# A fused transformer block on one core: cross attention written out head by head, x's tiles turned tile by tile at the layer borders, and the memory and bias transfers cut into pieces

## The reference, cut to what matters

```python
x = x + rms_norm(mixed, mix_post_g[l])
h = rms_norm(x, cross_pre_g[l])
m = rms_norm(mem, mem_norm_g[l])
qx = (h @ w_cq[l]).reshape(B, S, CX_HEADS, CX_HEAD_DIM)        # 4 heads of 128
kv = (m @ w_ckv[l]).reshape(B, M, 2, CX_HEADS, CX_HEAD_DIM)    # keys, values
s = jnp.einsum('bqhd,bkhd->bhqk', qx, kv[:, :, 0]).astype(jnp.float32) * CX_HEAD_DIM ** -0.5
p = jax.nn.softmax(s, axis=-1)
o = jnp.einsum('bhqk,bkhd->bqhd', p.astype(x.dtype), kv[:, :, 1]).reshape(B, S, CX_WIDTH)
x = x + rms_norm(o @ w_co[l], cross_post_g[l])
h = rms_norm(x, ffn_pre_g[l])
```

## Time and profile before

| what | us |
|---|---|
| median of 3 runs (2542.57 to 2543.47) | 2543.34 |
| the profiled execution | 2544.24 |
| its span, first to last instruction | 2542.4 |
| PE busy | 2493.5 (98%) |
| DVE busy | 1422.9 |
| ACT busy | 1222.6 |
| POOL busy | 23.3 |

### The profile page before, as it was taken

The page is one execution under the profiler, slowest core; times in us unless marked ns, Lnnn a source line. Parts: engine busy times, 40 slices in busy tenths (PEclk is TensorE's granted clock), DMA queues, the critical chain, the costliest instruction groups (busy, mean ns, idle before and its releaser), DMA issues.

```text
span 2542.4 us, 32059 instructions
## 1 busy us (share of the span) xinstructions
PE 2493.5 (98%) x11995; PEld 2080.1 (82%) x11995; DVE 1422.9 (56%) x1921; ACT 1222.6 (48%) x1699; POOL 23.3 (1%) x43
## 2 busy tenths in 40 slices
PE   8999999998999999999999999999999999999998
PEld 6788887877888888888888898887888888888887
DVE  4468887664645455454445655676654544544444
ACT  5645457654544444444445555554544444443443
POOL 1000000000000000000000000000000000000000
PEclk9999999997999999999999999999999999999999
DMA  7855444552556556655564775333565555556664
GB/s 239 244 178 159 151 145 158 165 190 85 187 186 190 188 190 190 190 186 194 191 196 150 229 222 177 105 123 127 161 196 189 190 190 190 190 186 207 195 191 157
DMA packets 238580, 456.07 MB, mean 179 GB/s; under 512 B 16468, under 2 KB 24916, under 8 KB 237712
## 3 DMA queue, kind: packets, MB, share of 16 engines
q1 hardware_dynamic: 234896, 440.92, 54.3%
q0 software_dynamic: 3584, 13.79, 1.8%
HBM read 449.40 MB, written 5.24 MB: 179 GB/s over the span
## 4 chain that ended last, share of the span: by engine, by line
PE 93%; DVE 3%; DMA 1%; ACT 1%; issue 1%; POOL 0%; DVEq 0%; ACTq 0%; POOLq 0%
PE g L310 23%; PE g L312 23%; PE g L311 23%; PE g L953 4%; PE g L955 4%; PE g L954 4%; PE g L1864 1%; DMA raw<-in_w_in 1%; PE g L1866 1%; PE g L1868 1%; PE m L983 1%; DVE wl L298 1%; PE m L706 1%; PE m L616 1%; ACT wh L294 0%
## 5 line engine op out<-in xcount | busy, mean ns | idle before, releaser
L298 DVE TENSOR_TENSOR wl<-raw,wh 128x1024 fp32r<-128x1024 f32 (+1 forms) x836 | 1015.1, 1220 | 939.4 <-ACT wh L294 936.5
L294 ACT ACTIVATE wh<-raw 128x1024 fp32r<-128x1024 f32 (+1 forms) x836 | 879.0, 1056 | 1114.6 <-PE g L312 919.8
L310 PE MATMUL g<-wh,act_hi 128*128 128x512 f32 x1824 | 720.0, 395 | 9.6 <-DVE wl L298 4.6
L311 PE MATMUL g<-wl,act_hi 128*128 128x512 f32 x1824 | 713.6, 391 | 0.0
L312 PE MATMUL g<-wh,act_lo 128*128 128x512 f32 x1824 | 713.5, 391 | 0.0
L310 PEld LDWEIGHTS g<-wh,act_hi 128*128 128x128 f32 x1824 | 344.6, 189 | 83.3 <-DVE act_lo L643 5.5
L312 PEld LDWEIGHTS g<-wh,act_lo 128*128 128x128 f32 x1824 | 344.7, 189 | 73.0
L311 PEld LDWEIGHTS g<-wl,act_hi 128*128 128x128 f32 x1824 | 345.1, 189 | 69.9
L310 PE MATMUL g<-wh,ht_hi 128*128 128x512 f32 x688 | 267.8, 389 | 0.0
L312 PE MATMUL g<-wh,ht_lo 128*128 128x512 f32 x688 | 267.7, 389 | 0.0
L311 PE MATMUL g<-wl,ht_hi 128*128 128x512 f32 x688 | 267.6, 389 | 0.0
(11 more groups left out here) (363 smaller groups left out, 2188.6 us busy)
## 6 DMA issues: line engine op xcount, KB each, us to landing
raw<-in_w_ffn_in SPq DMA_DIRECT2D x176, 512.0 KB, 3.4
raw<-in_ffn_w_in SPq DMA_DIRECT2D x176, 512.0 KB, 3.5
raw<-in_w_in SPq DMA_DIRECT2D x112, 512.0 KB, 4.3
raw<-in_w_ffn_out SPq DMA_DIRECT2D x88, 512.0 KB, 3.7
raw<-in_ffn_w_out SPq DMA_DIRECT2D x88, 512.0 KB, 3.6
raw<-in_nsa_w_in SPq DMA_DIRECT2D x80, 512.0 KB, 4.4
raw<-in_w_out SPq DMA_DIRECT2D x32, 512.0 KB, 4.6
raw<-in_nsa_w_out SPq DMA_DIRECT2D x32, 512.0 KB, 4.6
```

Of the source, the lines that this page charges most:

```text
L294: nc.scalar.activation(wh[:, j % SLOTS, 0:n], raw[:, j % SLOTS, 0:n], ACT.Copy).then_inc(hi_done, 1)
L298: nc.vector.tensor_tensor(wl[:, j % SLOTS, 0:n], raw[:, j % SLOTS, 0:n], wh[:, j % SLOTS, 0:n].bitcast(F32), ALU.subtract).then_inc(lo_don ...
L310: nc.tensor.matmul(dst, h, whk, start=(first and k == 0), stop=False)
L311: nc.tensor.matmul(dst, h, wlk, start=False, stop=False)
```

## The change

1. **Order of mx.** The query units are now 108 to 115, between the values' 104 to 107 and 116 to 119 (`CW_0`). x's first bank is transposed after unit 106 and not after 107; ACT's squares of x come after its conversion of unit 116.
2. **Queries** are multiplied with the weights stationary (24 matmuls of 256 columns a unit), so that they come out transposed; x's norm goes into the scale of the exponential. x's second half has its own tiles `xt_hi`, `xt_lo`.
3. **Cross attention** is written out for four heads without a loop and without POOL. Keys are transposed after unit 92, scores come behind unit 116, the softmax runs beside units 117 to 119, the values are multiplied so that co's operand comes out directly, and DVE writes the value rows of p1 ahead of its conversions of co's units.
4. **Borders.** Turned tiles of x go on one by one: PE waits for the first tile's high part and then for its low part (`pe_first_unit`, at in1f, ff1, in2c, ff2); the two tiles stand in different PSUM banks (`turn_rows`). co and fo1 are skewed as well; ACT squares tile 0 while tile 1 is multiplied, and loads the table of the square root ahead.
5. **Transfers.** `mem` comes in 4 pieces of 512 KB, the masks behind them, the bias rows are written in 12 pieces of 256 KB; each piece waits for a unit of in1q or mx. ACT's squares of `mem` move to units 26 and 27 of in1q.

```diff
+        def act_last_squares(act, name, junk, then, early):
+
+            s = gemms[name]
+            c = s["chunks"] - 1
+            for j in range(early):
+                act_unit(act, gemms[then]["u0"] // SLOTS, j)
+            for t in range(T):
+                act.wait_ge(*((tile_used, SKEWED[name]) if t == 0 else (unit_used, used(s, c))))
+                nc.scalar.activation(junk[:, c % 2, t, :], g[:, 2 * (c % 2) + t, :], ACT.Square, accum_out=ss8[:, t, c:c + 1])\
+                  .then_inc(ss_done, 1)
+                if t == 0:
+                    for j in range(early, AHEAD):
+                        act_unit(act, gemms[then]["u0"] // SLOTS, j)
...
-            u0 = s["units"] - SLOTS
+            n = min(SLOTS, s["units"])
+            u0, end = s["units"] - n, s["u0"] + s["units"] * s["chunks"]
             for t in range(T):
-                for j in range(SLOTS):
-                    slot = (s["u0"] + s["units"] * s["chunks"] - SLOTS + j) % SLOTS
-                    pe.wait_ge(lo_done, SLOTS + s["u0"] + s["units"] * s["chunks"] - SLOTS + j + 1)
...
+        def pe_first_unit(pe, name, cyc, hi, lo):
+
+            pe.wait_ge(lo_done, SLOTS + cyc * SLOTS + 1)
+            for k in range(2):
+                whk, wlk = wh[:, 0, k * NB:(k + 1) * NB], wl[:, 0, k * NB:(k + 1) * NB]
+                pe.wait_ge(*((first_hi, FIRST[name] + 1) if k == 0 else (hi_evac, BANKS[name] + 1)))
+                for t in range(T):
+                    h = hi[:, k, t * P:(t + 1) * P]
+                    nc.tensor.matmul(g[:, t, :], h, whk, start=(k == 0), stop=False)
+                    nc.tensor.matmul(g[:, t, :], h, wlk, start=False, stop=False)
+                pe.wait_ge(*((first_lo, FIRST[name] + 1) if k == 0 else (lo_evac, BANKS[name] + 1)))
+                for t in range(T):
+                    ins = nc.tensor.matmul(g[:, t, :], lo[:, k, t * P:(t + 1) * P], whk, start=False, stop=False)
+            ins.then_inc(unit_used, 1)
+
...
 
+        def turn_rows(name, b, k):
+
+            bank = BANKS[name] + b + (2 if k and b == 0 and name in FIRST else 0)
...
+                    26: mem_squares_first, 27: mem_squares(1, junk_m1), 29: lambda: act_sqrt(act, "nmem")}
...
+            if c == CQ:
+                for k in range(2):
+                    x_hi, x_lo = (tile_of("ncx", b, 2 * u + k) for b in (act_hi, act_lo))
+                    for h in range(CX_H):
+                        w0 = k * NB + h * P
+                        dst = g[:, 2 * (c % 2) + h // 2, h % 2 * S:(h % 2 + 1) * S]
+                        nc.tensor.matmul(dst, wh[:, n % SLOTS, w0:w0 + P], x_hi, start=(2 * u + k == 0 and h % 2 == 0), stop=False,
+                                         skip_group_check=True)
+                        nc.tensor.matmul(dst, wl[:, n % SLOTS, w0:w0 + P], x_hi, start=False, stop=False, skip_group_check=True)
+                        ins = nc.tensor.matmul(dst, wh[:, n % SLOTS, w0:w0 + P], x_lo, start=False, stop=(2 * u + k == 15),
+                                               skip_group_check=True)
...
+            pe_cx_keys(pe)
+            for n in range(O1_0 + 5, CV_0 + 3):
+                pe_mx_unit(pe, n)
+            pe.wait_ge(cx_keyed, 2)
+            pe_turn_bank(pe, "ncx", 0)
+            pe_mx_unit(pe, CV_0 + 3)
+            pe_turn_bank(pe, "ncx", 1)
             for j in range(8):
-                if j + 5 < 8:
-                    pe_turn_bank(pe, "ncx", j + 5)
                 pe.wait_ge(lo_evac, BANKS["ncx"] + j + 1)
                 pe_mx_unit(pe, CQ_0 + j)
+                if j + 2 < 8:
+                    pe_turn_bank(pe, "ncx", j + 2)
+            pe_mx_unit(pe, CW_0)
+            for h in range(CX_H):
+                pe_cx_scores(pe, h)
+            for n in range(CW_0 + 1, MX_UNITS):
+                pe_mx_unit(pe, n)
+            for h in range(CX_H):
+                pe_cx_back(pe, h)
+            for h in range(CX_H):
+                pe_cx_values(pe, h)
...
+            act_mx_unit(act, CW_0)
             act.wait_ge(x_done, ADDED["ncx"][1] + 16)
-            act_squares(act, "ncx", x, [junk_x[:, 0, :], junk_x[:, 1, :]])
-            act_mx_unit(act, CQ_0 + 4)
...
+            act_mx_unit(act, CW_0 + 2)
             act_sqrt(act, "ncx")
-            act_mx_unit(act, CQ_0 + 6)
-            act_mx_unit(act, CQ_0 + 7)
-            ahead(act_unit, act, "co")
-            act_mx_evict(act, CQ, MX_UNITS - 1)
-            act_unit(act, gemms["co"]["u0"] // SLOTS, AHEAD)
+            act_cx_queries(act)
+            act_mx_unit(act, CW_0 + 3)
+            act_unit(act, gemms["co"]["u0"] // SLOTS, 0)
+            for h in range(CX_H):
+                act_cx_exp(act, h)
+            for j in (1, 2):
+                act_unit(act, gemms["co"]["u0"] // SLOTS, j)
+            for h in range(CX_H):
+                act_cx_weights(act, h)
...
-        cx_banks, cx_q, cx_k, cx_qk, cx_p, cx_w = [m, g], [xq_s, xq_s1], [xk_s, xk_s1], [xqk, xqk1], [xp, xp1], [xpt, xpt1]
+            dve_cx_scale(dve)
+            dve_mx_unit(dve, CW_0 + 3)
+            dve_cx_top(dve, 0)
+            dve_cx_top(dve, 1)
+            dve_cx_soft(dve, 0)
+            dve_cx_top(dve, 2)
+            dve_cx_soft(dve, 1)
+            dve_cx_top(dve, 3)
+            dve_cx_soft(dve, 2)
+            dve_cx_soft(dve, 3)
+            dve_cx_rows(dve)
+            ahead(dve_unit, dve, "co")
+            for h in range(CX_H):
+                dve_cx_lo(dve, h)
+            dve_unit(dve, gemms["co"]["u0"] // SLOTS, AHEAD)
...
-        def pool_cx(pool):
-            pool.wait_ge(pair_free[CQ % 2], mx_pair[CQ % 2] + CQ // 2 + 2)
-            pool.wait_ge(pair_free[CKV_V % 2], mx_pair[CKV_V % 2] + CKV_V // 2 + 2)
-            with pool.Fori(0, CX_H // 2) as i:
...
-            for l in LANES:
-                pe.sem_inc(cx_turned[l], 1)
-            with pe.Fori(0, CX_H // 2) as i:
...
+            pe.wait_ge(pair_free[0], mx_freed(8))
+            pe.wait_ge(da_at, DA_H)
+            for h in range(CX_H):
+                for t in range(T):
+                    o1 = h % 2 * S + t * P
+                    ins = nc.tensor.transpose(m[:, KEY_BANK[h // 2], o1:o1 + P], p1[:, t, KV + h * P:KV + (h + 1) * P], ident[:, :])
...
+        def pe_cx_back(pe, h):
+            pe.wait_ge(cx_soft, T * (h + 1))
...
+        def pe_cx_values(pe, h):
+            pe.wait_ge(pair_free[CKV_V % 2], mx_freed(CKV_V))
+            pe.wait_ge(cx_kept, h + 1)
+            for k in range(2):
+                v = p1[:, k, KV + NB + h * P:KV + NB + (h + 1) * P]
+                ins = nc.tensor.matmul(m[:, h, 0:S], v, cx_pt[h][:, k, :], start=(k == 0), stop=(k == 1))
...
+        def act_cx_queries(act):
+            act.wait_ge(unit_used, mx_used(CW_0 - 1))
+            nc.scalar.activation(cx_qt[:, 0:2, :], g[:, 0, :].rearrange("p (h n) -> p h n", h=2), ACT.Copy).then_inc(cx_asked, 1)
+            nc.scalar.activation(cx_qt[:, 2:4, :], g[:, 1, :].rearrange("p (h n) -> p h n", h=2), ACT.Copy).then_inc(cx_asked, 1)
+            act.wait_ge(cx_asked, 2)
+            nc.scalar.activation(st[:, 251:252], neg_lam, ACT.Exp).then_inc(pair_free[CQ % 2], 1)
...
+        def act_cx_exp(act, h):
+            act.wait_ge(cx_topped, h + 1)
...
+        def dve_cx_top(dve, h):
+            n = slice(T * h, T * (h + 1))
+            dve.wait_ge(cx_scored, h + 1)
+            nc.vector.tensor_reduce(cx_top[:, n], m[:, h, :].rearrange("p (t n) -> p t n", t=T), X, ALU.max, negate=True)\
...
+        def dve_cx_soft(dve, h):
+            n = slice(T * h, T * (h + 1))
+            dve.wait_ge(cx_exped, T * (h + 1))
...
+        def dve_cx_rows(dve):
+            dve.wait_ge(unit_used, mx_used(MX_UNITS - 1))
+            for t in range(T):
+                ins = nc.vector.tensor_scalar(p1[:, t, KV + NB:KV + 2 * NB], g[:, 2 * (CKV_V % 2) + t, :],
+                                              rstd("nmem")[:, t:t + 1], None, ALU.mult)
+            ins.then_inc(pair_free[CKV_V % 2], 1)
...
+            in1q_0 = gemms["in1q"]["u0"]
+            for q in range(4):
+                pool.wait_ge(lo_done, SLOTS + in1q_0 + 2 + 4 * q)
+                pool.dma_start(memx[:, :, q * NB:(q + 1) * NB], a["mem"].rearrange("(t p) d -> p t d", p=P)[:, :, q * NB:(q + 1) * NB])\
+                  .then_inc(mem_in, 16)
+            pool.wait_ge(lo_done, SLOTS + in1q_0 + 18)
             pool.dma_start(masks[:, :], a["c_masks"]).then_inc(masks_in, 16)
-            pool.dma_start(memx[:, :, :], a["mem"].rearrange("(t p) d -> p t d", p=P)).then_inc(mem_in, 16)
...
+            for n in range(BIAS_PARTS):
+                pool.wait_ge(lo_done, SLOTS + in1q_0 + 22 + 3 * n)
+                rows = bt[2 * n:2 * n + 2, :]
+                skewed = bass.AP(tensor=rows.tensor, offset=rows.offset + P - 1, ap=[list(rows.ap[0]), [-1, P], [1, S]])
+                pool.dma_start(dram_bias[2 * n:2 * n + 2], skewed).then_inc(bt_stored, 16)
+            pool.wait_ge(bt_stored, 16 * BIAS_PARTS)
...
```

(7 more changed lines are left out.)

304 lines of the change are left out of this document (143 added, 161 removed).

## The result

| | us | ratio to before |
|---|---|---|
| before, median of 12 runs | 2543.27 (2542.12 to 2544.65) | |
| the changed kernel, median of 12 runs | 2527.38 (2524.19 to 2538.65) | 0.9945 [0.9934, 0.9957] |
| forecast | 2509.2, range 2502 to 2519 | |

The account below looks back on a forecast made before the run. PE bounds the kernel, busy 2493.5 of 2542.4 us, so gains come only from its idle time and lower-clock stretches. Transfers 6.0, cross attention 22.5 and borders 5.6 sum to 34.1 us: 2543.3 − 34.1 = 2509.2, range 2502 to 2519.

Parts of the forecast that it names:

- The rate of the whole write: Bias rows written in one go take 28.0 us; at that rate each of 12 pieces was to take 2.3 us.
- The price by the rule for small transfers: Skill's bandwidth rule, taken as half rate: a bias piece 4.7 us, a weight unit beside it 9.0, same result.
- The rest of the change: Everything but the transfers: cross attention with the new mx order 22.5 us and borders 5.6, a gain of 28.1.
- the transfer term: in1q, 86 to 97 us: cutting transfers removes PE's 4.35 us idle and 1.65 of half clock, together 6.0 us.
- (a): Rival at the transfers: pieces still starve PE and the whole 6.0 us stay, 2515.2 us; chance 0.07.
- (c): Slower rival: each of 16 pieces stalls PE 6.0 us, 2611 us; sign turns at 1.8 us a piece; chance 0.03.
- The new order of mx and cross attention: mx to co's start: PE's waits shrink, co starts at 576.2 instead of 598.98; 22.5 us, bounds 15 and 25.
- The borders: First units and chain at section borders: 5.6 us saved in sum, bounds 2.5 and 9.
- the chain: Chain to the first block after co and fo1: skewing and early table load save 0.5 us at each border, 1.0.
- the first units: in1f, ff1, in2c, ff2: PE waits for one turned tile's part; 0.9 us twice and 1.4 twice, 4.6.
- The bound of 9: Upper bound of the border term: half-clock stretches of 6.7 us at two borders shrink by half, 2 x 1.7.
- (d): Rival at the borders: the clock hides the tile-wise handover and nothing of 5.6 us remains, 2514.8 us; chance 0.07.

Follow-up runs that it names:

- e1: Changed kernel with the 12 bias pieces each cut across all 24 heads instead of two neighbouring rows: 2503.45 us, ratio 0.9846.
- e8: Kernel before with only the change's transfers, bias pieces of two neighbouring rows as in the change: 2558.18 us, ratio 1.0062.
- e7: Kernel before with only the change's transfers, but bias pieces cut across all 24 heads: 2535.28 us, ratio 0.9972.
- e9: The kernel of e1 (changed kernel, bias pieces across all 24 heads) run once more as yardstick: 2503.18 us.
- e4: Changed kernel with the bias rows in six 512 KB pieces of four neighbouring rows, one in six units: 2578.4 us, ratio 1.0139.
- e3: Changed kernel with its two-row bias pieces issued one in five units instead of one in three: 2526.09 us, ratio 0.9933.

## Why the prediction was wrong, step by step

**The step that failed** is "At the rate of the whole write a bias piece takes 28.0/12 = 2.3 us, so a weight unit beside it lands in about 6.6, under 8.2. I take all 6.0." A piece took 15.8 us and a weight unit beside it 8.7. The rate of the whole write came from moving 24 rows at once, and I kept it for a piece of two neighbours. The price by the rule for small transfers, which I weighed beside it, missed as well: the size wasn't the trouble (e1 has the same size, and its pieces take 4.8 to 5.3 us, near the estimate of 4.7), which rows go together was. The term was +6.0 in the forecast and is −15.8 as the change has it (e8): 21.8 us, more than the whole miss of 18.2. The rest of the change gave about 4 more than its forecast of 28.1 (32.1, e7 to e9), which hid a part of that. In the form of e1 the transfer term is +7.1 (e7), so for pieces that keep the form of the whole the reasoning from PE's idle time and the clock behind it holds. Even there the two numbers of the step are off, and in opposite directions: a piece takes about 5 us and not 2.3, and a weight unit beside it the usual 4.3 and not 6.6.

**Rivals.** (a), the pieces still starve PE, had the right mechanism but the old stall as its ceiling, and it argued with the bytes per us of the rings; the rings had room (156 GB/s in that stretch, where 312 were moved in one of before), and the loads were late all the same. (c), the slower side, also had this mechanism: its turning point was 1.8 us for each of 16. Measured, mem's four cost nothing and the twelve others 1.9 each (e8 − e7, 22.9 in all), under what everything else saves; in e4 six cost 12.5 each (75 in all), and there the sign turned. A chance of 0.07 and 0.03 for the two was too little for a transfer whose form no row of before showed.

**The new order of mx and cross attention**: forecast 22.5, measured 21.4 as the rest of e7 to e9 (32.1 − 9.6 − 1.1, and so only as good as four medians are; e7's runs span 5.5), and 22.35 between the same two points of the two traces. No run changes it alone. Not all inside was right, so that the sum came so close is partly luck. The scores waited 0.17 us for the queries and not 0.7. PE idles for 0.4 and not some 4 us between the last value unit and co (9.51 of 9.90 busy), since the weights' transposes and the products lie there head by head; so the granted clock stayed full, 1.00, where I had it fall. co's first matmul came 6.0 us behind the last value unit (591.2 to 597.18), forecast 7.

**The borders**: the chain 1.1 for 1.0 (not told from scatter), the first units 9.6 for 4.6. The waits were sized rightly (4.9 in the two traces); left out were the half-clock stretches that get shorter with them, at ff1, in2c and also at in1f, where I had counted only the wait. The bound of 9 had named this for two of them: "one of the 6.7 us stretches at half clock at the two borders shrinks by half each". In e9 both did, to 3.4; in the profiled execution of the changed kernel only the second one. (d) fell.

**Still open.** Why the changed kernel's executions scatter over 14 us. Pieces that hold up weights at each of twelve places make it plausible (e1 scatters over 2 in four runs), but e3 and e8 have pieces of the same rows and scatter over 2.3 and 3.5, though with four runs each against twelve, so it isn't explained. And whether the slow pieces are slow by their source partitions, by their closed place in DRAM, or by both.

## What to carry to other kernels

Before cutting a DMA into pieces, ask along which dimension: let each piece keep the rows (partitions) that the whole had, and cut the other dimension. A piece of a few neighbouring rows can be slow and, worse, make loads of other queues late; so judge it by what the loads beside it take. When a wait at a low clock goes, count the stretch at half clock behind it as well, for it can be worth as much as the wait.
